# Hybrid attention and pooling block on one core: half of v with the gate columns as the first projection, in token tiles, and the mixer's fills placed anew

## The reference

```python
a = rmsnorm(h, ln_mix[i]);  z = a @ w_in[i]
q, k, v, g_out, g_lr, u = jnp.split(z, splits, axis=-1)          # 256, 256, 512, 512, 16, 512 columns
gk = jax.nn.log_sigmoid(g_lr @ w_gate_lr[i] + b_gate[i]) / GLA_GATE_NORM
o = gla_chunked(q, k, v, gk)                                     # 4 heads, causal, with decay per key channel
o = rmsnorm(o, gla_norm[i]) * jax.nn.silu(g_out)
y_pool = multiscale_pool(u, w_pool[i], pool_scale[i])            # trailing windows 2, 4, 8, 16
h = h + jnp.concatenate([o, y_pool], axis=-1) @ w_out[i]
f = rmsnorm(h, ln_ffn[i])
h = h + (jax.nn.silu(f @ w_ffn_gate[i]) * (f @ w_ffn_up[i])) @ w_ffn_down[i]
e = rmsnorm(h, ln_ple[i])
h = h + jax.nn.sigmoid(e @ w_ple_gate[i]) * (p[i] @ w_ple_proj[i])
return rmsnorm(h, ln_final)
```

## Time and profile before

| | us |
|---|---|
| median of 3 runs | 1195.35 (1193.75 to 1197.02) |
| the profiled execution, its time | 1195.73 |
| its span, first to last instruction | 1193.8 |
| PE busy in the span | 1152.9 |
| DVE, POOL, ACT busy | 647.8, 578.5, 406.7 |

### The profile page before, as it was taken

The page is one execution under the profiler, slowest core; times in us unless marked ns, Lnnn a source line. Parts: engine busy times, 40 slices in busy tenths (PEclk is TensorE's granted clock), DMA queues, the critical chain, the costliest instruction groups (busy, mean ns, idle before and its releaser), DMA issues.

```text
span 1193.8 us, 15018 instructions
## 1 busy us (share of the span) xinstructions
PE 1152.9 (97%) x5592; PEld 953.5 (80%) x5592; DVE 647.8 (54%) x750; ACT 406.7 (34%) x634; POOL 578.5 (48%) x369
## 2 busy tenths in 40 slices
PE   6999999999999989999999999999999999899994
PEld 4788899778788768888888888888888888778883
DVE  6446568525754963545454545454545454884435
ACT  6331112135334543333333333333333332464422
POOL 2111245503313776656565656565656565781103
PEclk9998999999999989999999999999999999999997
DMA  6211100201401111111111111111111110501003
GB/s 234 88 36 36 37 22 16 72 1 71 161 16 36 38 65 56 54 50 52 51 51 51 53 51 53 52 51 52 52 50 54 51 52 17 193 1 44 9 1 141
DMA packets 22695, 67.76 MB, mean 57 GB/s; under 512 B 2418, under 2 KB 3331, under 8 KB 20611
## 3 DMA queue, kind: packets, MB, share of 16 engines
q1 hardware_dynamic: 22658, 67.26, 15.9%
HBM read 63.06 MB, written 4.19 MB: 56 GB/s over the span
## 4 chain that ended last, share of the span: by engine, by line
PE 38%; POOL 28%; issue 23%; DVE 7%; ACT 1%; DMA 1%; POOLq 1%; SPq 0%; DVEq 0%; ACTq 0%
POOL r_lo L534 17%; PE pb L1443 10%; PE pb L1445 10%; PE pb L1444 10%; POOL raw_b L552 4%; POOL raw_a L550 3%; POOL s_sum L545 2%; POOL raw_a L548 2%; PE pb L1564 2%; DVE t_raw L1258 1%; PE pb L1545 1%; PE pb L1544 1%; DVE e_lo L961 1%; DVE sums L971 1%; DVE h L1324 1%
## 5 line engine op out<-in xcount | busy, mean ns | idle before, releaser
L471 POOL TENSOR_TENSOR w_lo<-w_raw,w_hi 128x2048 fp32r<-128x2048 f32 (+1 forms) x12 | 56.5, 4710 | 202.2 <-ACT w_hi L611 202.2
L534 POOL TENSOR_TENSOR r_lo<-raw_b,r_hi 128x512 fp32r<-128x512 f32 x66 | 96.0, 1454 | 101.2 <-ACT r_hi L738 101.2
L1324 DVE TENSOR_TENSOR h<-h,pb 128x512 f32<-128x512 f32 x176 | 116.6, 681 | 50.8 <-PE pb L1445 49.7
L1632 PE MATMUL pb<-t_hi,r_hi 128*128 128x512 f32 x352 | 137.9, 392 | 0.0
L1633 PE MATMUL pb<-t_lo,r_hi 128*128 128x512 f32 x352 | 137.3, 390 | 0.0
L1634 PE MATMUL pb<-t_hi,r_lo 128*128 128x512 f32 x352 | 137.0, 389 | 0.0
L534 POOL TENSOR_TENSOR r_lo<-raw_a,r_hi 128x512 fp32r<-128x512 f32 x66 | 89.8, 1362 | 94.0 <-ACT r_hi L738 94.0
L1443 PE MATMUL pb<-gu_hi,r_hi 128*128 128x512 f32 x320 | 124.5, 389 | 0.0
L1444 PE MATMUL pb<-gu_lo,r_hi 128*128 128x512 f32 x320 | 124.5, 389 | 0.0
L1445 PE MATMUL pb<-gu_hi,r_lo 128*128 128x512 f32 x320 | 124.5, 389 | 0.0
L1632 PE MATMUL pb<-b_hi,r_hi 128*128 128x512 f32 x264 | 104.5, 396 | 6.0 <-ACT c_s L773 3.6
(11 more groups left out here) (203 smaller groups left out, 2629.0 us busy)
## 6 DMA issues: line engine op xcount, KB each, us to landing
raw_d<-in_w_ffn_down_dram SPq DMA_DIRECT2D x22, 512.0 KB, 3.5
w_raw<-in_w_in_dram SPq DMA_DIRECT2D x8, 1024.0 KB, 5.5
raw_a<-in_w_ffn_gate_dram SPq DMA_DIRECT2D x11, 512.0 KB, 3.3
raw_b<-in_w_ffn_gate_dram SPq DMA_DIRECT2D x11, 512.0 KB, 4.2
raw_a<-in_w_ffn_up_dram SPq DMA_DIRECT2D x11, 512.0 KB, 3.8
raw_b<-in_w_ffn_up_dram SPq DMA_DIRECT2D x11, 512.0 KB, 4.6
h<-in_x_t_dram SPq DMA_DIRECT2D x16, 256.0 KB, 6.7
w_raw<-in_w_out_dram SPq DMA_DIRECT2D x4, 1024.0 KB, 5.8
```

The lines of the kernel that those rows point to most:

```text
L471: nc.gpsimd.tensor_tensor(w_lo[s][:, 0:size], w_raw[s][:, 0:size], w_hi[s][:, 0:size].bitcast(F32), ALU.subtract).then_inc(w_lo_ready[s], 1)
L534: nc.gpsimd.tensor_tensor(r_lo[q % RING][:].rearrange("p (k n) -> p k n", k=kts), src, r_hi[q % RING][:].bitcast(F32).rearrange("p (k n) - ...
L1324: V.tensor_tensor(h[:, m, both(c)], h[:, m, both(c)], aux.bank(F_DOWN + n)[:], ALU.add).then_inc(aux.drained, 1)
L1632: M(bank[:], wh[:, k, :], x_h[:, k, :], start=start and k == 0, stop=False, skip_group_check=True)
```

## The change

Block 0 is now the first half of v, and the 16 gate columns stand beside it in one operand of 272 columns (`v_raw`, `v_hi`, `v_lo`). It is projected in token tiles, one bank to a tile: 24 matmuls of 128 x 272 for each of 8 tiles (`v_token_tile`), four ahead of each half of k. The two units of the gate columns and their tile of weights are gone. DVE drains a tile as 256 columns of `v_tok` and 16 of `lr_tok`; a new fill `lrt` transposes the latter back (8 transposes), DVE copies them (`lr`), and `gate` waits for that. SP loads the weights in two halves of the contraction, each as 1 KB and 64 byte pieces, and the token loads stand around them in another order. POOL makes the low part of the first half, DVE that of the second. There are 8 blocks where there were 9: 5 is the other half of v, 6 and 7 are the output gate. Every fill and every step of the window sums has a new place, and POOL makes the last two window sums one behind the other, between `block_lo(5)` and `block_lo(6)`. In the final norm DVE no longer adds the last square (PE takes it in the column sums) and no longer builds a diagonal ahead of the spread (PE broadcasts the factors against the identity).

```diff
-BLOCKS_IN = [(OFF_LR, 1), (KEY, 2), (0, 2), (OFF_U, 2), (OFF_U + BW, 2), (OFF_V, 2), (OFF_V + BW, 2), (OFF_G, 2),
-             (OFF_G + BW, 2)]
-NB = len(BLOCKS_IN)
+BLOCKS_IN = [(OFF_V, 2), (KEY, 2), (0, 2), (OFF_U, 2), (OFF_U + BW, 2), (OFF_V + BW, 2), (OFF_G, 2), (OFF_G + BW, 2),
+             (OFF_LR, 1)]
+NB = len(BLOCKS_IN) - 1
...
-FILLS_AFTER = {(1, 3): [("gate", n) for n in range(4)], (2, 3): [("dec", n) for n in range(4)]}
-FILLS_AFTER[3, 1] = [("diag", 0)]
+FILLS_AFTER = {(1, 2): [("lrt", 0), ("lrt", 1)] + [("gate", n) for n in range(4)], (2, 1): [("dec", n) for n in range(4)]}
+FILLS_AFTER[2, 3] = [("diag", 0)]
...
-FILLS_AFTER[6, 2] = [("near", 0)]
-for _j in range(4):
-    FILLS_AFTER[7, _j] = ([("kt", 2 * _j), ("kt", 2 * _j + 1)] if _j < 2 else [("kv", 2 * _j - 4), ("kv", 2 * _j - 3)]
-                          ) + [("y", 2 * _j), ("y", 2 * _j + 1)]
-FILLS_AFTER[8, 0] = [("o", n) for n in range(4)]
-FILLS_AFTER[8, 1] = [("o", n) for n in range(4, 8)]
-FILLS_AFTER[8, 2] = [("ot", n) for n in range(4)]
+    FILLS_AFTER[3 + _lev // 2, 2 * (_lev % 2) + 1] = [(_lev, n) for n in range(4)]
+FILLS_AFTER[6, 0] = [("near", 0)]
+FILLS_AFTER[6, 1] = [("y", 0), ("y", 1)]
+FILLS_AFTER[6, 2] = [("kt", n) for n in range(4)]
+FILLS_AFTER[6, 3] = [("kv", 0), ("kv", 1), ("y", 2), ("y", 3)]
+FILLS_AFTER[7, 0] = [("kv", 2), ("kv", 3), ("y", 4), ("y", 5)]
+FILLS_AFTER[7, 1] = [("o", n) for n in range(4)] + [("y", 6), ("y", 7)]
+FILLS_AFTER[7, 2] = [("o", n) for n in range(4, 8)]
+FILLS_AFTER[7, 3] = [("ot", n) for n in range(4)]
...
+            def v_load(half):
+                kts = slice(half * HK, (half + 1) * HK)
+                for col, at_in, wide, used in ((0, BLOCK_AT[0], BW, BW), (BW, BLOCK_AT[NB], P, RANK)):
+                    src = w_in[:, at_in:at_in + KT * wide].rearrange("p (k n) -> p k n", k=KT)
+                    sp.dma_start(v_raw[:, kts, col:col + used], src[:, kts, 0:used]).then_inc(v_landed[half], 16)
...
+            x_load(0)
+            sp.dma_start(gains_all[:], gains_in).then_inc(small_landed, 16)
+            v_load(0)
+            for n in range(1, 4):
+                x_load(n)
+            v_load(1)
+            for n in range(4, 8):
+                x_load(n)
+            block_load(1)
+            sp.dma_start(ident[:], consts[:, 0:P]).then_inc(ident_landed, 16)
+            for n in range(8, 16):
+                x_load(n)
             block_load(2)
...
+            pool.wait_ge(first_hi, 1)
+            nc.gpsimd.tensor_tensor(v_lo[:, 0:HK, :], v_raw[:, 0:HK, :], v_hi[:, 0:HK, :].bitcast(F32), ALU.subtract
+                                    ).then_inc(first_lo, 1)
+            for b in range(1, 5):
                 block_lo(b)
             pool.wait_ge(mixer_landed, 16 * 3)
             windowed(0)
             windowed(1)
+            block_lo(5)
+            windowed(2)
+            windowed(3)
             block_lo(6)
...
+                if n in (1, 4):
+                    half = n // 4
+                    kts = slice(half * HK, (half + 1) * HK)
+                    act.wait_ge(v_landed[half], 32)
+                    nc.scalar.copy(v_hi[:, kts, :], v_raw[:, kts, :]).then_inc(first_hi, 1)
                 act.wait_ge(x_landed[n], 16)
                 hi_tile(n, 0, 0, a_hi, x_hi_done)
-            half = KT * BW // 2
-            act.wait_ge(w_landed[1], 16)
-            nc.scalar.copy(w_hi[1][:, 0:half], w_raw[1][:, 0:half]).then_inc(first_hi, 1)
-            nc.scalar.copy(w_hi[1][:, half:], w_raw[1][:, half:]).then_inc(w_hi_ready[1], 1)
             for n in range(KT):
                 square(n, n, 0, x_sq, x_sum)
+                if n == 3:
+                    block_hi(1)
             for n in range(KT, 16):
-                if n == 12:
+                if n == 10:
                     root(0, 0)
                 act.wait_ge(x_landed[n], 16)
                 hi_tile(n - KT, 1, 0, a_hi, x_hi_done)
                 square(n, n - KT, 1, x_sq, x_sum)
+            block_hi(2)
             root(0, 1)
...
+            exp_diff(2)
             for b in range(4, 7):
                 block_hi(b)
-                exp_diff(2 * b - 6)
                 exp_diff(2 * b - 5)
-            block_hi(7)
+                if b < 6:
+                    exp_diff(2 * b - 4)
...
+                if n == 5:
+                    dve.wait_ge(first_hi, 2)
+                    V.tensor_tensor(v_lo[:, HK:KT, :], v_raw[:, HK:KT, :], v_hi[:, HK:KT, :].bitcast(F32), ALU.subtract
+                                    ).then_inc(v_lo_rest, 1)
                 dve.wait_ge(x_landed[n], 16)
                 lo_tile(n, n, 0, 0, a_hi, a_lo, x_hi_done, x_lo_done)
...
+            def v_tile(u, t):
                 dve.wait_ge(proj.filled, u + 1)
-                V.tensor_tensor(lr[0:RANK, both(c)], proj.bank(u)[0:RANK, :], rms_all[0:RANK, both(c)], ALU.mult
+                V.tensor_scalar(v_tok[:, t, 0:BW], proj.bank(u)[:, 0:BW], stat[:, 3, t:t + 1], None, ALU.mult
+                                ).then_inc(lr_part, 1)
+                V.tensor_scalar(lr_tok[:, t, :], proj.bank(u)[:, BW:VW], stat[:, 3, t:t + 1], None, ALU.mult
                                 ).then_inc(proj.drained, 1)
...
+            for n in range(KT, 16):
+                if n == 8:
+                    norm_var(F_NORM1, 0)
+                if n == 10:
+                    first_recip(0)
+                    dve.wait_ge(ident_landed, 16)
+                    first_diag(0)
+                    for t in range(4):
+                        v_tile(t, t)
+                if n == 13:
+                    norm_take(F_NORM1, 0)
+                    dve.wait_ge(aux.drained, F_NORM1 + 2)
+                    tile_unit(4, Z_K, 0)
+                if n == 15:
+                    tile_unit(5, Z_K + 1, 0)
+                dve.wait_ge(x_landed[n], 16)
+                lo_tile(n, n - KT, 1, 0, a_hi, a_lo, x_hi_done, x_lo_done)
+                add_squares(n, n - KT, 1, x_sq, x_sum)
             norm_var(F_NORM1, 1)
-            norm_diag(0, 1)
-            norm_take(F_NORM1, 1)
+            first_recip(1)
+            first_diag(1)
...
+            drains_after(1, 2)
+            tile_unit(11, Z_K + 1, 1)
             for j in range(4):
                 tile_unit(u_in(2) + j, Z_Q + j // 2, j % 2)
-                if j == 1:
+                if j == 0:
                     dve.wait_ge(soft_ready, 3)
                     V.scalar_tensor_tensor(out=soft[:], in0=pre[:], scalar=0.0, in1=soft[:], op0=ALU.min,
                                            op1=ALU.subtract).then_inc(log_ready, 1)
+                if j == 1:
+                    drains_after(2, 1)
+                    dve.wait_ge(aux.drained, FILL["dec", 3] + 1)
+                    dve.wait_ge(x_lo_done, 16)
+                    level_diff(0)
+            dve.wait_ge(proj.drained, u_in(3))
+            qk_product()
             drains_after(2, 3)
-            dve.wait_ge(aux.drained, FILL["dec", 3] + 1)
-            dve.wait_ge(proj.drained, u_in(3))
-            dve.wait_ge(x_lo_done, 16)
-            level_diff(0)
-            qk_product()
+            level_diff(1)
+            level_scale(0)
...
-                    if (b, j) in ((5, 1), (5, 3), (6, 1), (6, 3)):
-                        pooled(((5, 1), (5, 3), (6, 1), (6, 3)).index((b, j)))
-                    if (b, j) == (7, 0):
+                    if (b, j) in ((3, 3), (4, 1), (4, 3), (5, 2)):
+                        pooled(((3, 3), (4, 1), (4, 3), (5, 2)).index((b, j)))
+                    if (b, j) == (6, 1):
...
+                    if n < 15:
+                        add_squares(n, *ple_tile(n), y_sq, y_sum)
             norm_var(F_NORM4, 1)
-            norm_diag(3, 1)
+            dve.wait_ge(root_ready, 8)
+            V.reciprocal(stat[:, 3, 4:8], stat[:, 1, 4:8]).then_inc(recip_ready, 1)
...
+                if kind == "lrt":
+                    for j in range(4):
+                        i = nc.tensor.transpose(bank[0:RANK, j * P:(j + 1) * P], lr_tok[:, 4 * n + j, :], ident[:])
...
+            def v_token_tile(u, t, first):
+                rows = slice(t * C, (t + 1) * C)
+                for k in range(KT):
+                    if t % 4 == 0:
+                        pe.wait_ge(x_lo_done, KT * (t // 4) + k + 1)
+                    if first and k == HK:
+                        pe.wait_ge(v_lo_rest, 1)
+                    i = split3(proj.bank(u)[:, 0:VW], a_hi[:, k, rows], a_lo[:, k, rows], v_hi[:, k, :], v_lo[:, k, :],
+                               k == 0, k == KT - 1)
+                i.then_inc(proj.filled, 1)
+            pe.wait_ge(first_lo, 1)
             pe.wait_ge(ones_ready, 5)
             for c in range(NC):
-                proj.claim(3 * c)
-                unit(3 * c, w_hi[0], w_lo[0], 1, 0, a_hi, a_lo, c, ready=lambda k: pe.wait_ge(x_lo_done, KT * c + k + 1))
+                for t in range(4 * c, 4 * c + 4):
+                    proj.claim(t + 2 * c)
+                    v_token_tile(t + 2 * c, t, t == 0)
```

(48 more changed lines are left out.)

143 lines of the change are left out of this document (60 added, 83 removed).

## The result

The changed kernel takes 1206.41 us (median of 4 runs, 1205.50 to 1210.36) against 1195.91 us of the kernel before. The ratio is 1.0101, with a 95% interval of 1.0079 to 1.0122, so it is slower. The forecast of 1202.1 was 4.3 us too low; 1206.4 lies in its range (1190 to 1209) and in the likeliest case's own (1197 to 1208). The profiled execution took 1205.50 us with a span of 1203.7, 9.9 us more than the span of before.

The account below looks back on a forecast made before the run. The prediction took PE's own instruction sequence to bound the kernel (PE busy 97% of the span). Costs of 22.7 us against 15.9 us saved gave +6.8 us on 1195.73, 1202.5, put at 1202.1 for the median; range 1190 to 1209.

Parts of the forecast that it names:

- the likeliest case: Whole kernel: added waits, tiles and half-clock time of 22.7 us outweigh 15.9 us saved, net +6.8 us, 1202.1; 40% chance.

## What to carry to other kernels

Where an edit takes a unit of PE work from between a producer and its consumer, follow every handover for a unit and a half behind it, not the first alone: each shared resource (here the time of GpSimd's 4.6 us instructions against DVE's) meets another partner. Here GpSimd's long instructions did least harm where DVE drained PSUM, and the engine that releases them (here ScalarE's rounding) is where this was set. A change that is sound can measure slower by its seams alone: this one was 1% slower as it stood and 0.9% faster with some twenty lines in another order. Of that 0.9%, one line's worth is no merit of the change: the kernel before gains 0.3% by it too.
